# The additions of the norms' squares on GpSimd instead of VectorE

## The reference, cut to what matters

```python
def layer_norm(x, g, b):
    xf = x.astype(jnp.float32)
    mu = jnp.mean(xf, -1, keepdims=True)
    var = jnp.mean(jnp.square(xf - mu), -1, keepdims=True)
    return ((xf - mu) * lax.rsqrt(var + LN_EPS) * g + b).astype(x.dtype)

def trunk_layer(x, mods, mixer, ln_g, ln_b, w1, w3, w2):
    ...
    x = layer_norm(DN_ALPHA * x + g1 * out, ln_g[0], ln_b[0])
    x = layer_norm(DN_ALPHA * x + g2 * swiglu(modulate(x, sh2, sc2), w1, w3, w2), ln_g[1], ln_b[1])
```

## Time and profile before

| | |
|---|---|
| time, median of 3 runs | 1916.07 us (1911.18 to 1919.71) |
| profiled execution: its time, its span | 1910.98 us, 1909.2 us |
| busy: PE, DVE, ACT, POOL | 1708.8, 953.8, 580.8, 233.5 us |
| additions of squares (L820) on DVE | 7 on SQA, 21 on SQB |
| mean granted clock of PE, share of full speed | 0.928 |

### The profile page before, as it was taken

One profiled execution on the slowest core, in us unless ns is written; L12 is line 12 of the kernel. 1 busy time (PEld: TensorE's weight loads), 2 busy tenths in 40 slices (PEclk: granted clock), 3 DMA queues, 4 the chain that ended last, 5 costly groups with the idle time before them and its releaser, 6 DMA issues. The chain is left out here.

```text
span 1909.2 us, 29584 instructions
## 1 busy us (share of the span) xinstructions
PE 1708.8 (90%) x11660; PEld 1565.7 (82%) x11660; DVE 953.8 (50%) x1732; ACT 580.8 (30%) x906; POOL 233.5 (12%) x219
## 2 busy tenths in 40 slices
PE   5797897979999999999798655899979999999996
PEld 2695344979999999999698205899979999999996
DVE  0336666787654575355853892132574232233248
ACT  2224565244322232223442114232244212221221
POOL 0000121332351153111021012000000000000000
PEclk8797999979999999999795677999979999999997
DMA  6531563412442344333177474522222222222212
GB/s 245 103 100 39 202 211 126 95 43 67 138 127 81 110 134 128 92 102 105 45 197 178 147 231 109 139 77 77 69 64 76 78 78 77 67 77 78 61 50 56
DMA packets 273184, 204.36 MB, mean 107 GB/s; under 512 B 30840, under 2 KB 238832, under 8 KB 273072
## 3 DMA queue, kind: packets, MB, share of 16 engines
q1 hardware_dynamic: 238656, 161.40, 29.3%
q10 hardware_dynamic: 27632, 24.72, 4.5%
q0 software_dynamic: 6784, 16.66, 3.3%
HBM read 178.10 MB, written 24.64 MB: 106 GB/s over the span
## 5 line engine op out<-in xcount | busy, mean ns | idle before, releaser
L470 PE MATMUL PS<-XH,WH 128*128 128x320 f32 x2112 | 488.8, 313 | 28.9 <-DVE XL L1045 12.8
L470 PE MATMUL PS<-XL,WH 128*128 128x320 f32 x2112 | 485.7, 311 | 0.0
L470 PE MATMUL PS<-XH,WL 128*128 128x320 f32 x2112 | 485.0, 311 | 0.0
L470 PEld LDWEIGHTS PS<-XH,WH 128*128 128x128 f32 x2112 | 357.1, 190 | 30.5 <-issue 27.4
L435 ACT ACTIVATE WH<-RAW 128x1024 fp32r<-128x1024 f32 x188 | 198.6, 1057 | 555.8 <-PE PS L470 542.2
L470 PEld LDWEIGHTS PS<-XL,WH 128*128 128x128 f32 x2112 | 357.8, 190 | 0.0
L470 PEld LDWEIGHTS PS<-XH,WL 128*128 128x128 f32 x2112 | 357.1, 190 | 0.0
L687 DVE TENSOR_TENSOR HT<-PS,GT 128x640 f32<-128x640 f32 x52 | 42.9, 825 | 423.2 <-PE PS L470 421.2
L440 DVE TENSOR_TENSOR WL<-RAW,WH 128x1024 fp32r<-128x1024 f32 x188 | 243.1, 1316 | 9.3 <-ACT WH L435 7.9
L470 PE MATMUL PS<-HH,WH 128*128 128x320 f32 x832 | 190.4, 310 | 0.0
L470 PE MATMUL PS<-HL,WH 128*128 128x320 f32 x832 | 189.6, 309 | 0.0
(11 more groups left out here) (252 smaller groups left out, 1733.0 us busy)
## 6 DMA issues: line engine op xcount, KB each, us to landing
RAW<-in_ffn_w SPq DMA_DIRECT2D x120, 512.0 KB
RAW<-in_w_ada SPq DMA_DIRECT2D x96, 512.0 KB
c_scratch<-G ACTq DMA_DIRECT2D x32, 256.0 KB, 3.4
b_scratch<-BP ACTq DMA_DIRECT2D x16, 512.0 KB, 2.7
BT<-b_scratch POOLq DMA_DIRECT2D x8, 1024.0 KB, 5.4
RAW<-in_ssm_w_glu SPq DMA_DIRECT2D x16, 512.0 KB
CPL<-c_scratch SPq DMA_DIRECT2D x8, 1024.0 KB, 5.5
RAW<-in_ffn_w SPq DMA_DIRECT2D x16, 384.0 KB
```

The source lines that it names most:

```text
L470: ins = nc.tensor.matmul(PS[:, 2 * u + h, 0:HALF], w[:, u, k, :], m[:, k, HALF * h:HALF * h + HALF], start=start, stop=stop)
```

## The change

add_square and its calls leave dve_residual_norm. A new function pool_squares(g, q) does the same seven additions on POOL, with the same waits and the same semaphores. Its four calls stand in POOL's stream ahead of pool_inputs (norm 0), behind all pool_powers (norm 1), behind the wait for the state-space outputs (norm 2) and at the end (norm 3).

```diff
@@ dve_residual_norm
-            def add_square(k):
-                v.wait_ge(ln_sq, KT * q + k + 1)
-                v.wait_ge(ln_sqsum, 7 * q + k - 1) if 7 * q + k > 1 else None
-                total = squares(q)[:, 2, :]
-                v.tensor_tensor(total, total, squares(q)[:, k % 2, :], ALU.add).then_inc(ln_sqsum, 1)
...
             center(5)
-            add_square(1)
-            add_square(2)
...
             center(6)
-            add_square(3)
-            add_square(4)
...
             center(7)
-            add_square(5)
-            add_square(6)
             v.wait_ge(ln_cent, KT * q + 8)
             residual(7)
             add_to_sum(7).then_inc(ln_sum, 1)
-            add_square(7)
             split(2)
+
+        def pool_squares(g, q):
+            total = squares(q)[:, 2, :]
+            for k in range(1, KT):
+                g.wait_ge(ln_sq, KT * q + k + 1)
+                if 7 * q + k > 1:
+                    g.wait_ge(ln_sqsum, 7 * q + k - 1)
+                g.tensor_tensor(total, total, squares(q)[:, k % 2, :], ALU.add).then_inc(ln_sqsum, 1)
...
             pool_ssm_start(g)
+            pool_squares(g, 0)
             pool_inputs(g)
             for b in range(ITEMS):
                 pool_powers(g, b)
+            pool_squares(g, 1)
             pool_ssm(g)
             g.wait_ge(fin_out, 32)
+            pool_squares(g, 2)
             g.wait_ge(psum_free, BASE["wout"] + 8)
...
+            pool_squares(g, 3)
```

## The result

The changed kernel takes 1920.82 us (median of 20 runs, 1916.45 to 1928.43). The kernel before, over 20 runs of its own, takes 1911.80 (1905.35 to 1919.71): the ratio is 1.0049, with an interval from 1.0037 to 1.0061. So the change costs about 9 us, close to half a per cent of the time (the interval reaches from 0.37 to 0.61 per cent). The forecast time, 1920.8, was met; the forecast *effect*, +4.7, was not: the median of the three runs that the prediction started from lay 4.3 above that of 20 runs, and this hid about half of the real effect.

What follows compares the result with a forecast made beforehand. PE was taken as the bound (busy 90%), DVE counting only where PE stands still in the norms. Norms 0 to 3 gave 1.2 + 1.5 + 1.4 + 0.6 = 4.7, on 1916.07: 1920.8, range 1911 to 1930.

Steps and rivals of the forecast that it cites:

- Mechanism: DVE additions with both inputs in SBUF and POOL operations exclude each other for a whole instruction; waiting engines take turns.
- Rival (a): In the norms, both engines run without holding each other and DVE simply loses the additions: -7.5, to 1908.6; chance 0.07.
- Price of an addition: One 640-column addition on POOL holds 1.42, or takes 1.55 with its start; bounds of the hold 1.15 and 2.23.
- Rival (b): In the norms, POOL becomes the chain because an addition holds 1.8 to 2.23: up to +18, 1934; chance 0.11.
- Norm 2: Third norm: residual(7) waits for PE anyway, so only the last addition, losing to the split, counts: +1.4.
- Norm 0: First norm: L637 starts 2.9 earlier, but pool_inputs then collides with the small steps: +1.2, between -2.4 and +3.5.
- Norms 1 and 3: Second and last norm: additions hold some of DVE's centerings, corrections and splits: +1.5 and +0.6.
- additions 5 and 6 run under residuals and cost nothing: In norm 3, without splits, these two additions fall beside DVE's residuals and cost 0; additions 1, 2 and 4 cost 1.4 each.
- 6 costs 0.1: In norm 1, the sixth addition delays DVE by only 0.1, of 5.8 for the first six.
- POOL wakes 0.16 after ACT's result: Delay from ACT's finished result to POOL's start, read from the trace in norm 0: 0.16.
- Net 0: Layer 0's feed-forward net, between norm 0 and norm 1: no change forecast, 0.
- paragraph on queues: Work behind POOL's and ACT's new waits, including pool_inputs delayed by about 11, is not needed soon and costs nothing.

Runs made afterwards that it cites:

- write_only: Changed kernel with each POOL addition replaced by a memset of the total that reads nothing, so the variance is wrong; 1906.41 us, ratio 0.9976 to the kernel before.
- inputs_late: Changed kernel with pool_inputs also waiting until norm 0's last low part (XL) is made; 1922.46 us, ratio 1.0063 to the kernel before.
- norm3_only: Kernel before with the seven additions moved to POOL in norm 3 alone; 1916.5 us, ratio 1.0027.
- polite: Changed kernel with POOL's additions of blocks 4 to 6 also waiting for DVE's next centering; 1911.68 us, ratio 1.0009 to the kernel before.
- after_again: Changed kernel run once more, unchanged, for a second profile; 1926.97 us in one run.
- norm0_only: Kernel before with the seven additions moved to POOL in norm 0 alone, ahead of pool_inputs; 1912.62 us, ratio 1.0004.
- late_split: Changed kernel with DVE's third split waiting for the last addition of squares in norms 0 to 2; 1917.43 us, ratio 1.0034 to the kernel before.
- before_again: Kernel before run once more, unchanged, for a second profile; 1911.67 us in one run.
- norms13_polite: Kernel before with additions on POOL in norms 1 and 3 only, those of blocks 4 to 6 waiting for the next centering; 1910.68 us, ratio 1.0009.
- all_three: Changed kernel with the waits of polite, late_split and inputs_late together; 1913.85 us, ratio 1.0007 to the kernel before.

## Why the prediction was right, and where not

- **Mechanism: right.** POOL's additions and DVE's two-input instructions exclude each other, and an instruction with an input in PSUM runs on (1.26 and 1.14 beside POOL, everywhere). Rival (a), free running, is excluded by the rows; write_only, 4.6 below the kernel before by its ratio, shows about what it would have looked like.
- **Price of an addition: right.** 1.53 to 1.59 where it isn't held, forecast 1.55. Rival (b) needed a hold above 1.85 for half a per cent. That hold did not occur, though what the rival concluded from it, that additions hold DVE again and again, came true in norm 3 at the lower price.
- **Norm 2: right** (+1.5 for +1.4). What DVE loses early goes into the wait for PE; the tail costs 1.4. The split came first, by a small margin, as walked.
- **Norm 0: right** (+0.9 for +1.2). L637 began 2.9 earlier measured from the norm's first mean, as forecast, and pool_inputs then took the gain back under the small steps. The changed kernel's rows answer to the walk behind the earlier trace rows (L937 is now the subtraction, L930 to L932 the NS steps). DVE:

```profile
406.53 1.12 DVE L937 TENSOR_TENSOR X<-X,ACC 128x640 f32<-128x640 f32 x1 [2.84 <-ACT ACC L959]
407.79 2.08 DVE L930 TENSOR_TENSOR NS<-NS 128x5 f32<-128x5 f32 x1
409.91 0.17 DVE L931 TENSOR_TENSOR NS<-NS 128x5 f32<-128x5 f32 x1
410.11 1.78 DVE L932 SCALAR_TENSOR_TENSOR NS<-NS 128x5 f32<-128x5 f32 x1
```

and POOL:

```profile
405.04 1.93 POOL L1449 TENSOR_TENSOR BB<-BB,AC 128x1024 f32<-128x1024 f32 x1
407.05 2.80 POOL L1450 TENSOR_TENSOR BB<-BB,BW 128x1024 f32<-128x1024 f32 x1
409.93 1.94 POOL L1451 TENSOR_TENSOR BB<-BB,AC 128x1024 f32<-128x1024 f32 x1
```

  Two steps on five columns, 0.17 alone, take 2.08 and 1.78, while the one between them slips in: this is the forecast's pattern, instruction by instruction. inputs_late confirms its price: without pool_inputs there the norm is 3.9 shorter.
- **Norms 1 and 3: wrong**, and this is the step that failed. The prediction put for norm 3: "additions 5 and 6 run under residuals and cost nothing", and for norm 1: "6 costs 0.1". It doesn't print each turn, but both come out with its "POOL wakes 0.16 after ACT's result", and so does its addition 5 of norm 1, which loses to a split and then holds center(6). The 0.16 is from one row, of another pair of instructions. In the norms POOL wakes 0.08 after ACT, and the race between square plus wake (0.74 + 0.08) and L810 with its gap (0.82 + 0.04) goes to POOL by 0.04 each time; with 0.16 it would have gone to DVE by the same 0.04. The 31 us for which POOL had been idle in that row are not the reason: norm 3's first addition, behind 467.51 of idle time, also started 0.08 after its square. Why that row has 0.16 stays open. The walk had been tested on the old order to within 0.35, nine times the margin that decided. Two more centerings are hit in norm 3 (2 x 1.37 = 2.7) and one in norm 1 (1.35): added to the forecast's +0.6 and +1.5 this makes 3.3 and 2.9, and 3.4 and 2.7 were measured. In norm 3 the agreement is in part luck: L637 begins 4.4 later, not 3.3, and then takes 0.9 less, two effects of PE's clock that nearly cancel (last section). norm3_only and polite show the step from both sides: alone it costs the whole 3.4, and with the race decided the other way norms 1 and 3 gain.
- **Net 0: forecast at nothing, +4.1 in the profiled execution.** The prediction's paragraph on queues gave the late pool_inputs no cost, and PE's waits bear it out: PE is idle in net 0 for 6.1 before and 6.6 after, nearly all of it for POOL's powers (6.1 and 6.4). But its products, the same in number, take 479.0 instead of 475.3. A wait of PE for the powers in the kernel before, and the one at the same place in the changed kernel:

```profile
733.32 1.09 PE L1550 MATMUL PS<-IDENT,BP 128*128 128x128 f32 x8 [2.48 <-POOL BP L1533]
736.37 1.92 PE L1545 MATMUL PS<-IDENT,BP 128*128 128x128 f32 x8 [2.16 <-POOL BP L1528]
```

  and the 4 us from there on, before and after (PE's instructions stand in the first brackets, its granted clock third from the end):

```profile
733.32:737.32 4.00, 4.00 (x29) 4.00 (x30) 0.00 (x0) 1.49 (x5) 0.00 (x0) 1.00 0.80 242
736.37:740.37 4.00, 4.00 (x19) 4.00 (x20) 0.17 (x1) 1.49 (x5) 0.00 (x0) 0.57 0.78 213
```

  At 0.57 instead of 1.00 these 4 us cost 1.7. The 4 us behind another wait (3.84, to 537.71) are at 0.60 and cost 1.6; the two make 3.3 of the 3.7. Behind waits for the powers there are two such stretches in after, after_again, norm0_only and late_split (net 0 of 483.7 to 485.5), one in before_again, norm3_only and polite (481.3 to 481.5), and none in before, write_only and norms13_polite (481.4, 482.1 and 479.3). inputs_late has none there and all_three two, and both have one more behind PE's wait for a split. The late pool_inputs stands in all with two, but in polite, write_only and inputs_late as well, so that it brings them about isn't shown. Nor does the length of the wait alone decide: 2.48 is followed by none, 2.16 by one. What decides stays open. The norms' +8.5 alone nearly give the medians' +9.0; norm0_only's interval of 0.0018 to either side, some 3.5 us, can't tell 2.5 from nothing.
- **The range: right, its lower end badly added.** 1916.07 less 1.3 and 4.9 is 1909.9 and not 1911, and its own terms (3.6 in norm 0, twice 1.08) give -1.1 and not -1.3. Nothing hangs on it here.

So the forecast time came out for two wrong reasons that cancel: an effect that was 4 too small, on a starting median 4 too high.

## What to carry to other kernels

In these traces work moved from VectorE to GpSimd is not off VectorE's time while both read SBUF: it costs the two-input instruction that it meets nearly its own length (1.3 to 1.4 for an addition of 1.53 to 1.59), and 28 additions taken away left the engine busy for longer. What decides is which instruction it meets, so look for the instructions that don't contend (an input in PSUM, as the residuals have) and put the GpSimd operation under those by an explicit wait, instead of leaving it to a race. Where such a race is closer on paper than the walk's own error (0.35 here), give both outcomes, and multiply by how often the order repeats; and where work is only put off, look at what it meets at its new place.

## What the runs showed that I had not expected

**A race of 0.04 us is stable.** For blocks 5 and 6 of norm 1 and 4 to 6 of norm 3 POOL won by 0.04 to 0.05 each time, in both runs of the changed kernel and in norm3_only; the stretches repeat within 0.11.

**PE's granted clock in the small sums goes both ways.** In norm 2, the sum L633 starts behind the same idle time (2.28 or 2.29) in all twelve traces, and takes 1.28 to 1.30 in six of them, 1.45 in one (write_only) and 2.19 to 2.30 in the other five. The windows over that instruction (stretch, length, then PE busy and its instructions, PEld, DVE, ACT, POOL, the granted clock, the DMA share and GB/s), in the kernel before:

```profile
1399.30:1400.60 1.30, 1.27 (x12) 1.28 (x12) 1.30 (x2) 0.00 (x0) 0.84 (x2) 1.00 0.20 35
```

and in norm3_only, where norm 2 has the same code:

```profile
1401.70:1403.90 2.20, 2.20 (x11) 2.20 (x11) 1.83 (x2) 0.00 (x0) 0.79 (x2) 0.50 0.54 177
```

The clock is granted in full (2.4 GHz) in the one and by half (1.2 GHz) in the other, and this is the one difference that I found between norm 2's stretches of 43.1 (before) and 44.2 (norm3_only, norms13_polite). What decides it stays open. The same kernel can have either: behind the same 2.25 of idle time, L633 of norm 0 takes 2.27 in after and 1.25 in after_again. And norm 3 of norm0_only, whose code is that of before, took 43.35 instead of 44.26, because of this row of norm0_only, where the earlier trace rows have 2.16:

```profile
1894.10 1.25 PE L637 MATMUL PS<-MEANW,SQB 128*128 128x1 f32 x10
```

So a norm's stretch can move by about 1 us without a change in its code, and the differences of norms 1 to 3 stand because L637 already begins later there, by 2.7, 1.4 and 4.4. In norm 3 of the changed kernel the clock works both ways at once:

```profile
1896.70 4.48 PE L1825 MATMUL PS<-IDENT,X 128*128 128x128 f32 x24 [3.86 <-DVE X L814]
...
1902.05 1.25 PE L637 MATMUL PS<-MEANW,SQB 128*128 128x1 f32 x10
```

PE stood 3.86 for the late centering, and the transposes behind that ran at a granted clock of 0.56 in their first 2.5 us (1.00 before, behind no such wait; in polite, where PE waited 0.22, the same 24 take 2.81 instead of 4.48):

```profile
1896.70:1899.20 2.50, 2.50 (x13) 2.50 (x14) 1.97 (x5) 0.74 (x1) 0.51 (x1) 0.56 0.00 0
```

L637 then found the full clock, and took 1.25, where before it took 2.16 at 0.53. From the end of the last centering to the end of L637 it is 7.05 before and 6.75 after, so the centering's delay of 3.8 became the stretch's 3.4 to 3.5.
